# Differential attention: combine two probability maps before the turn, one turn and one value product a head

## The reference

```python
def blocked_attention(q, k, v, scale):      # per head
    s = einsum(q, k) * scale
    p = softmax(s, axis=-1)                 # 128 queries x 384 keys
    return einsum(p, v)

o_c = blocked_attention(q_c, k_c, v_c, ...) # 8 latent heads (MLA), values of width 64
o_d = blocked_attention(q_d, k_d, v_d, ...) # 4 differential heads, two maps each, values of width 128
lam = exp(sum(lp[0]*lp[1])) - exp(sum(lp[2]*lp[3])) + lam_init
o_d = rms_norm(o_d[:, :, 0] - lam * o_d[:, :, 1], subln_g) * (1.0 - lam_init)
out = concatenate([o_c, o_d]) @ w_out
```

## Time and profile before

| | |
|---|---|
| median of 3 runs | 1489.79 us (1488.0 to 1490.24) |
| profiled execution | 1489.46 us, span 1487.5 us |
| TensorE matmuls busy | 1311.6 us, 88% of the span |
| TensorE weight loads | 915.6 us, 62% |
| VectorE / ScalarE / GpSimd | 525.2 / 337.8 / 163.6 us |
| transfers | 345.75 MB, mean 232 GB/s |
| units 16 to 47 | about 1035 to 1123 us of the span |

### The profile page before, as it was taken

The page is one execution under the profiler, slowest core; times in us unless marked ns, Lnnn a source line. Parts: engine busy times, 40 slices in busy tenths (PEclk is TensorE's granted clock), DMA queues, the critical chain, the costliest instruction groups (busy, mean ns, idle before and its releaser), DMA issues.

```text
span 1487.5 us, 38763 instructions
## 1 busy us (share of the span) xinstructions
PE 1311.6 (88%) x16880; PEld 915.6 (62%) x16880; DVE 525.2 (35%) x1156; ACT 337.8 (23%) x671; POOL 163.6 (11%) x226
## 2 busy tenths in 40 slices
PE   5989999989999999999898669978899899988882
PEld 2448854468888547787676334545665578866651
DVE  1324444135456746111111053448455351111103
ACT  2223221142333123000000033433443220000001
POOL 2004310023343000000000030020000000000001
PEclk8999999999999998999999979978879899999996
DMA  9841157550111155999999881326314469999995
GB/s 398 310 164 60 60 195 237 174 205 9 54 60 60 58 203 221 356 387 391 397 405 418 362 318 57 113 73 226 114 57 170 175 230 378 400 395 394 392 426 193
DMA packets 39799, 345.75 MB, mean 232 GB/s; under 512 B 5611, under 2 KB 10555, under 8 KB 21360
## 3 DMA queue, kind: packets, MB, share of 16 engines
q1 hardware_dynamic: 21456, 302.11, 51.5%
q0 software_dynamic: 7104, 22.90, 4.7%
q10 hardware_dynamic: 11104, 18.75, 3.9%
HBM read 322.30 MB, written 21.45 MB: 231 GB/s over the span
## 4 chain that ended last, share of the span: by engine, by line
PE 65%; DMA 18%; issue 7%; DVE 6%; ACT 3%; ACTq 0%; DVEq 0%; POOLq 0%; POOL 0%; SPq 0%
PE PB L699 60%; DMA arena<-in_w_moe 15%; PE PB L702 6%; DVE arena L2037 3%; DMA ring<-in_w_mod 2%; ACT arena L1560 1%; DVE small L2050 1%; DMA expert_out<-arena 1%; DVE x L2037 1%; DVE arena L2044 0%; ACT hT L1560 0%; DMA arena<-expert_out,rows_i 0%; ACT L1560 0%; DVE arena L2047 0%; ACT ring L1560 0%
## 5 line engine op out<-in xcount | busy, mean ns | idle before, releaser
L699 PE MATMUL PB<-arena 64*64 64x64 f32 (+7 forms) x9524 | 477.1, 294 | 50.7 <-DMA arena<-in_w_moe 37.2
L699 PEld LDWEIGHTS PB<-arena 64*64 64x64 f32 (+3 forms) x9524 | 376.6, 130 | 146.2 <-issue 78.0
L699 PE MATMUL PB<-ring,hT 128*128 128x512 f32 (+1 forms) x720 | 314.0, 591 | 7.2 <-DVE hT L2040 3.6
L699 PEld LDWEIGHTS PB<-ring,hT 128*128 128x128 f32 x720 | 137.3, 194 | 167.2 <-issue 162.5
L699 PE MATMUL PB<-ring,arena 128*32 128x256 f32 (+2 forms) x3712 | 209.4, 380 | 9.9 <-DMA ring<-in_w_moe 7.0
L699 PEld LDWEIGHTS PB<-ring,arena 128*32 128x32 f32 x3712 | 172.4, 110 | 38.4 <-issue 9.9
L1560 ACT ACTIVATE arena<-PB 128x256 f32<-128x256 f32 (+3 forms) x217 | 106.4, 490 | 333.0 <-PE PB L699 279.5
L702 PE MATMUL PB<-cst,arena 128*128 128x128 f32 (+2 forms) x758 | 117.3, 296 | 42.5 <-ACT arena L1560 20.0
L702 PEld LDWEIGHTS PB<-cst,arena 128*128 128x128 f32 (+2 forms) x758 | 90.2, 155 | 88.1 <-issue 48.4
L2470 DVE TENSOR_TENSOR arena<-arena,PB 128x256 f32<-128x256 f32 (+1 forms) x32 | 15.1, 471 | 288.6 <-PE PB L699 168.5
L699 PE MATMUL PB<-ring,scT 128*32 128x512 f32 x384 | 60.8, 753 | 21.9 <-DMA ring<-in_w_mod 16.0
(11 more groups left out here) (148 smaller groups left out, 928.7 us busy)
## 6 DMA issues: line engine op xcount, KB each, us to landing
arena<-in_w_moe SPq DMA_DIRECT2D x50, 2048.0 KB, 24.5
ring<-in_w_moe SPq DMA_DIRECT2D x46, 2048.0 KB, 27.3
ring<-in_w_mod SPq DMA_DIRECT2D x24, 2048.0 KB, 8.5
ring<-in_w_mix SPq DMA_DIRECT2D x22, 2048.0 KB, 8.3
expert_out<-gate ACTq DMA_DIRECT2D x1, 3456.0 KB, 21.9
expert_out<-arena ACTq DMA_DIRECT2D x12, 288.0 KB
tokens<-arena ACTq DMA_DIRECT2D x6, 512.0 KB, 4.0
expert_out<-arena ACTq DMA_DIRECT2D x20, 128.0 KB
```

The lines of the kernel that those rows point to most:

```text
L699: return nc.tensor.matmul(out, lhsT, rhs, start=start, stop=stop, **k)
```

## The change

For the differential heads of tiles 1 and 2, the two exp results are combined on VectorE into one map (`combined(u)`, at the odd unit u), which is turned and multiplied with the values once. `TURNED` lists the units that are turned: all MLA units, and the odd differential units; `turned_last(u)` is the unit whose values are issued in iteration u, and is nothing at an odd differential u. The probabilities get four buffers of their own (`probs`, in space where the query weights had been), the sums eight columns instead of four. The turned and the product buffers alternate by the position in `TURNED`.

```diff
+        probs = u0.rearrange("p (b n) -> p b n", b=4)
+        TURNED = [u for u in range(16, 48) if u % 16 < 8 or u % 2]
+        PLACE_OF = {u: n % 2 for n, u in enumerate(TURNED)}
+        def turned_two_back(u):
+            n = TURNED.index(u)
+            return TURNED[n - 2] if n > 1 else None
+        def turned_last(u):
+            if u % 16 >= 8 and u % 2:
+                return None
+            return max([v for v in TURNED if v < u], default=None)
...
                 def turn(u):
-                    pe.wait_ge(*when("prob", u))
+                    pe.wait_ge(*when("comb" if u % 16 >= 8 else "prob", u))
...
                     if u % 2 == 0 and u + 2 < 48:
                         scores(u + 2)
                         scores(u + 3)
-                    turn(u)
-                    if u > 16:
-                        values(u - 1)
+                    if u in TURNED:
+                        turn(u)
+                    if turned_last(u):
+                        values(turned_last(u))
...
                         act.wait_ge(*when("nmax", u))
-                        if u >= 18:
-                            act.wait_ge(*when("pT", u - 2))
                         if u >= 20:
-                            act.wait_ge(*when("ov", u - 4))
+                            v = u - 4
+                            act.wait_ge(*when("pT", v) if v % 16 < 8 else when("comb", v) if v % 2 else when("pT", v + 1))
+                        if u >= 24:
+                            v = u - 8
+                            act.wait_ge(*when("ov", v) if v % 16 < 8 else when("comb", v + 1 - v % 2))
...
-                        if u > 16:
-                            weights_T(u - 1)
+                        if turned_last(u):
+                            weights_T(turned_last(u))
...
                     o = mix[t % 2][:, 512 + 128 * ((m - 8) // 2):640 + 128 * ((m - 8) // 2)]
-                    if m % 2 == 0:
-                        ts(o, PB[:, 4 + u % 2, 0:128], rec, None, ALU.mult, None, "ov", u)
-                    else:
-                        tt(rec, rec, small[:, 62:63], ALU.mult)
-                        stt(o, PB[:, 4 + u % 2, 0:128], rec, o, ALU.mult, ALU.add, "ov", u)
+                    ts(o, PB[:, 4 + b, 0:128], small[:, 248 + b:249 + b], None, ALU.mult, None, "ov", u)
+
+                def combined(u):
+                    sums = [small[:, 240 + v % 8:241 + v % 8] for v in (u - 1, u)]
+                    part, b = small[:, 68:69], PLACE_OF[u]
+                    dve.wait_ge(*when("prob", u))
+                    step(V.reciprocal(part, sums[1]))
+                    stt(part, part, sums[0], small[:, 62:63], ALU.mult, ALU.mult)
+                    step(V.reciprocal(small[:, 248 + b:249 + b], sums[0]))
+                    stt(probs[:, (u - 1) % 4, :], probs[:, u % 4, :], part, probs[:, (u - 1) % 4, :], ALU.mult, ALU.add, "comb", u)
...
                     if u + 2 < 48:
                         top(u + 2)
-                    if u > 16:
-                        out(u - 1)
+                    if u not in TURNED or u % 16 < 8:
+                        if turned_last(u):
+                            out(turned_last(u))
+                    else:
+                        combined(u)
```

More of the change, by code:

```diff
@@ L1384, in turn @@
                     n = operands(u)[3]
-                    pe.wait_ge(*when("prob", u))
-                    claim(2 + u % 2, "probT", u)
+                    pe.wait_ge(*when("comb" if u % 16 >= 8 else "prob", u))
+                    b, from_ = PLACE_OF[u], u - 1 if u % 16 >= 8 else u
+                    claim(2 + b, "probT", u)
                     for k in range(n):
-                        ins = tp(PB[:, 2 + u % 2, 128 * k:128 * k + 128], prob[:, u % 2, 128 * k:128 * k + 128])
+                        ins = tp(PB[:, 2 + b, 128 * k:128 * k + 128], probs[:, from_ % 4, 128 * k:128 * k + 128])
                     ins.then_inc(*tick("pe", "pT", u))
@@ L1393, in values @@
                     pe.wait_ge(*when("probT", u))
-                    claim(4 + u % 2, "ov", u)
+                    b = PLACE_OF[u]
+                    claim(4 + b, "ov", u)
                     w = 64 if units[u][1] < 8 else 128
                     for k, v in enumerate(vs):
-                        ins = mm(PB[:, 4 + u % 2, 0:w], probT[:, u % 2, k, :], v, k == 0, k == len(vs) - 1)
+                        ins = mm(PB[:, 4 + b, 0:w], probT[:, b, k, :], v, k == 0, k == len(vs) - 1)
                     ins.then_inc(*tick("pe", "pv", u))
@@ L1619, in weights_T @@
             def weights_T(u):
-                n = 384
+                n, b = 384, PLACE_OF[u]
                 act.wait_ge(*when("pT", u))
-                if u > 17:
-                    act.wait_ge(*when("pv", u - 2))
-                fn(probT[:, u % 2, :, :].rearrange("p k n -> p (k n)")[:, 0:n], PB[:, 2 + u % 2, 0:n], ACT.Copy, "probT", u)
+                if turned_two_back(u):
+                    act.wait_ge(*when("pv", turned_two_back(u)))
+                fn(probT[:, b, :, :].rearrange("p k n -> p (k n)")[:, 0:n], PB[:, 2 + b, 0:n], ACT.Copy, "probT", u)
             def heads_raw(n):
@@ L1983, in _ @@
                         act.wait_ge(*when("nmax", u))
-                        if u >= 18:
-                            act.wait_ge(*when("pT", u - 2))
                         if u >= 20:
-                            act.wait_ge(*when("ov", u - 4))
+                            v = u - 4
[3 more added lines that the diff above has]
+                            act.wait_ge(*when("ov", v) if v % 16 < 8 else when("comb", v + 1 - v % 2))
                         scale = (96 if m < 8 else 64) ** -0.5
-                        fn(prob[:, u % 2, 0:n], PB[:, SCORES[u % 4], 0:n], ACT.Exp, "prob", u,
-                           bias=small[:, 64 + u % 4:65 + u % 4], scale=scale, accum_out=small[:, 240 + u % 4:241 + u % 4])
-                        if u > 16:
-                            weights_T(u - 1)
+                        fn(probs[:, u % 4, 0:n], PB[:, SCORES[u % 4], 0:n], ACT.Exp, "prob", u,
+                           bias=small[:, 64 + u % 4:65 + u % 4], scale=scale, accum_out=small[:, 240 + u % 8:241 + u % 8])
+                        if turned_last(u):
+                            weights_T(turned_last(u))
                         if u in (17, 33):
@@ L2652, in out @@
                     dve.wait_ge(*when("pv", u))
-                    rec = small[:, 68:69]
-                    step(V.reciprocal(rec, small[:, 240 + u % 4:241 + u % 4]))
+                    b = PLACE_OF[u]
                     if m < 8:
-                        ts(mix[t % 2][:, 64 * m:64 * m + 64], PB[:, 4 + u % 2, 0:64], rec, None, ALU.mult, None, "ov", u)
+                        rec = small[:, 68:69]
+                        step(V.reciprocal(rec, small[:, 240 + u % 8:241 + u % 8]))
+                        ts(mix[t % 2][:, 64 * m:64 * m + 64], PB[:, 4 + b, 0:64], rec, None, ALU.mult, None, "ov", u)
                         return
                     o = mix[t % 2][:, 512 + 128 * ((m - 8) // 2):640 + 128 * ((m - 8) // 2)]
-                    if m % 2 == 0:
-                        ts(o, PB[:, 4 + u % 2, 0:128], rec, None, ALU.mult, None, "ov", u)
-                    else:
-                        tt(rec, rec, small[:, 62:63], ALU.mult)
-                        stt(o, PB[:, 4 + u % 2, 0:128], rec, o, ALU.mult, ALU.add, "ov", u)
+                    ts(o, PB[:, 4 + b, 0:128], small[:, 248 + b:249 + b], None, ALU.mult, None, "ov", u)
[7 more added lines that the diff above has]
+                    stt(probs[:, (u - 1) % 4, :], probs[:, u % 4, :], part, probs[:, (u - 1) % 4, :], ALU.mult, ALU.add, "comb", u)
                 def squares(t):
```

## The result

The changed kernel takes 1513.05 us (median of 4 runs, 1511.82 to 1515.42); the kernel before, on the same chip, 1488.89 us (4 runs). The ratio is 1.0177, with a 95% interval of 1.0157 to 1.0198: 24 us slower. The profiled execution took 1515.42 us, its span is 1513.6 us, 26.1 more than before.

The account below looks back on a forecast made before the run. TensorE was taken to bound the differential stretches before the change, a TensorE-VectorE loop after it: 1489.46 + 14.7 (loop at full clock) + 10 (lower clock) = 1514 us, range 1502 to 1522, likeliest 1508 to 1518.

Parts of the forecast that it names:

- TensorE was the bound at full clock: Differential heads before the change: TensorE goes on without real gap, 2.99 us a head, everything else fits beside it.
- The moved wait closes a loop: Differential heads: turn waits for combination, next scores queue behind it, VectorE needs them; 4.67 us a head, not 2.99.
- Both links that it named: Differential-head loop: scores queued behind the waiting turn, and VectorE's result, which needs the values, ahead of the next combination.
- Its exp has long been done.: Loop of a differential head: the next combination waits for no exp; ScalarE is free from 1.22, needs some 0.7.
- VectorE's durations: Per differential head: 384-column combination 0.62, one-column instruction with step 0.19, `combined` 1.19; VectorE's work 2.91 before, 3.14 after.
- Entries and ends: First turns of tiles: +2.7 at turn 25, +2.6 in tile 2; everything behind attention shifts one to one.
- The clock: Differential stretches: TensorE's new pauses make the granted clock alternate between its two levels, adding +10 us.
- a price of 16.6 at half clock all through: Differential stretches wholly at 1.2 GHz: 11.4 for the loops and some 5 for the rest, given as +16.6 us.
- a share of 62%: Time at 1.2 GHz, taken from 1036 to 1058, where several pauses gave a mean clock of 0.69.
- The pauses: TensorE stands about 2.6 us in each loop, four times as long as the 0.6 us pauses the clock got through.
- The case for the loop at full clock: Rival: loop closes but clock stays at 1.00, as from 1058 to 1084; +14.7 us, 1504; chance 20%.
- The first rival: TensorE stays the bound in differential heads, 8 x 1.00 us less, faster at 1481; chance 3%.

Follow-up runs that it names:

- experiment 10: Kernel before, with unread 512-column products (2, 1, 1, 2) issued ahead of the turns of units 18, 19, 21 and 34: 1475.59 us, ratio 0.9933.
- experiment 4: Changed kernel, with two unread 512-column products issued on TensorE ahead of each wait for a combination: 1496.95 us, ratio 1.0075.
- experiments 1 and 2: Changed kernel; first: next head's scores issued ahead of the waiting turn, 1502.7 us; second: a head's result put behind the next combination on VectorE, 1502.4 us.
- experiment 3: Changed kernel with both order changes, scores ahead of the waiting turn and result behind the next combination: 1496.9 us, ratio 1.008.
- experiment 8: Changed kernel with combined maps turned one unit later, tile 2's MLA and differential pairs alternating, five differential heads' results scaled on ScalarE: 1483.78 us, ratio 0.9984.
- experiment 6: Changed kernel with the turn of each combined map one unit later on TensorE, its copy and result moved along: 1489.71 us, ratio 1.0015.
- the interleaved kernels: Changed kernel with later turns and tile 2's MLA and differential pairs alternating: 1484.25 us; with five results on ScalarE 1483.78; with unread products added too 1480.09.

## Why the prediction was right

The prediction was 1514, measured are 1513.05, and its range and sign hold. Step by step:

- *TensorE was the bound at full clock.* Right, but only with the second half of the sentence: experiment 10 adds work to TensorE, in its pauses, and the kernel becomes faster, so the clock counts beside the work.
- *The moved wait closes a loop, 4.67 us a head at full clock.* Right. At a clock of 1.00 it is 4.87 (experiment 4); at the lower clock 6.58 was worked out and 6.66 measured (turn 41 to 43). Both links that it named were shown to be links by themselves (experiments 1 and 2, periods of 5.79 and 5.46 against 5.6 and 5.4 expected).
- *"Its exp has long been done."* True of the changed kernel, and so of the forecast. But it hid a third link, which appeared as soon as the other two were cut (experiment 3). For this reason, and for one late pair of scores, the sum for that experiment was too low by 0.5 to 1.5 a head.
- *VectorE's durations.* The 384-column combination was put at 0.62 and takes 0.618. The one-column `stt` was put at 0.16 and takes 0.219, and the steps between add a little: with its way to TensorE the combination takes 1.33 and not 1.24, half of the difference between 4.87 and 4.67. From turn 25 to 31 and from 41 to 47 the sum is 1 us too low in all at full clock (experiment 4).
- *Entries and ends.* +2.7 at turn 25 as forecast; the shift behind attention is one to one.
- *The clock.* Put at +10. Experiment 4 shows 9.3 in the loops, and at most 1.7 more lie outside them. That the sum comes so close is in part luck. The 10 was made of a price of 16.6 at half clock all through and a share of 62%, and the share was borrowed from a stretch of MLA units with other pauses; nothing in the trace before tied the two. (The parts of the 16.6, 11.4 and 5, make 16.4.) The windows of the differential heads, 0.68 and 0.67, are 64% and 66% of the time at the lower level. The mean hides what single loops do: one ran wholly at half clock (6.66), in another the clock came back within the loop (6.41, mean 0.74). The Trainium skill ("TensorE: Matmul & The Clock Gate", A second HAM failure mode) says that small idle times between groups of matmuls make the clock alternate between its two levels. The 0.68 and 0.67 of the windows agree with it.
- *The pauses.* The case for the loop at full clock named pauses of about 0.6 us that the clock got through between 1058 and 1084. There are longer ones in the same stretch: 1.26 us before the turn at 1060.18 and 1.25 before that at 1069.93, both with the clock at 1.00. The new pauses are twice as long as these, not four times.
- *The first rival*, TensorE stays the bound (1481), asked for scores that are issued ahead of the waiting turn. With that freedom, and the third link cut, its gain could still not be measured (0.9984, 0.9960 to 1.0007, in experiment 8). One reason is shown: where four differential heads follow one another, VectorE is the bound (experiment 6). What else takes up the 8 us was not taken apart. The Trainium skill ("Perfetto Trace Analysis", Identifying the Most-Contended Engine) says to optimize the engine with the highest occupancy first. Taken as the prediction's rival took it, for TensorE, that gave the wrong sign here, since the order of the instructions decided. The same section judges TensorE by its weight loads and not by its matmul busy time. By that measure TensorE has 11.64 of the 16 us in 1106 to 1122, and ScalarE 12.39.

Open: how the clock falls in the interleaved kernels and what unread products in tile 2 would bring them, and how much of the differences between single profiles in the MLA units is chance. The kernel before alone ran from 1478.6 to 1492.6 us on the later chips.

## What to carry to other kernels

When work moves to another engine, write down for each engine what stands behind the instruction that now waits. If that is something the other engine needs in order to go on, the engines take turns, and the time is the sum of their latencies, not the largest of their loads: here 4.87 us at full clock for 2.0 us of TensorE work. The remedy is an order in which the waiting instruction is issued one unit later on every engine that it passes (three here); cutting one link of a loop shows only the next one.

Where TensorE stops for a microsecond or two again and again, look at the granted clock before counting its work: here 9 us of a loss of 24, and the gain of 10 us that experiment 10 found in the kernel before, came with the clock.

## What was not expected of the hardware

- Products that nobody reads made a kernel faster: six products of 512 columns, 5.8 us of TensorE time, brought 0.67% (0.43 to 0.91) to the kernel before. In the changed kernel 32 recorded matmuls, 16.3 us, lay in waits (each turn behind them still waited 0.76 to 1.79 us for VectorE), and the clock in tile 2's heads was 1.00 in place of 0.67.
- A one-column `scalar_tensor_tensor` with two tensor inputs and a scalar takes 0.219 us, where a one-column reciprocal takes 0.16 and a one-column `tensor_scalar` 0.15 (the changed kernel, 8 of each kind or more).
- Two score products of 64 rows each, at partitions 0 and 64, have a reader, the first map's reduction, that starts 1.01 us behind their first load. The four recorded matmuls of both maps end 0.08 us ahead of it (1110.75, 0.92 us in all).
